# The first block by token halves, gathers of two slots for 64 tokens, and column pairs on TensorE

## Reference

```python
# first block, cut
h = rmsnorm(x, ln_mix_g) * (1 + sc1) + sh1
q, kc, vc, ksl, vsl, kw, vw, gts, cb, cc, ch = split(h @ w_in)
o_attn = nsa_mixer(...)                     # per query block: compressed, selected, window
o_conv = cb * causal_conv3(cc * ch)
mixed = concat([rmsnorm(o_attn, g), rmsnorm(o_conv, g)])
x = x + gt1 * (mixed @ w_out)
h2 = rmsnorm(x, ln_ffn_g) * (1 + sc2) + sh2
# peer_ffn(h2): q = h2 @ w_q; s = q . sub_keys  (8 heads x 2 halves x 128 keys)
# top 16 of each half, top 16 of their 256 sums -> expert number and softmax weight g
u = expert_u[ec]                            # 128 tokens x 128 slots x 1024
act = gelu(einsum('cd,ced->ce', xc, u))
out = einsum('ce,ced->cd', gc * act, expert_v[ec])
x = x + gt2 * out
# second block: attention with rotary embedding and a gated delta net, on the normed x
```

## Time and profile before

| | us |
|---|---|
| median of 3 runs (lowest, highest) | 1513.19 (1512.33, 1513.9) |
| the profiled execution, its own time | 1513.2 |
| its span, first to last instruction | 1511.3 |
| PE busy / DVE busy / ACT busy / POOL busy | 1281.6 / 746.8 / 477.1 / 368.4 |
| mean granted TensorE clock | 0.948 |

### The profile page before, as it was taken

How to read it: one execution, slowest core, us unless ns; L and a number is a source line. 1 busy time by engine, 2 the same in 40 slices (tenths; PEclk the granted TensorE clock), 3 DMA queues, 4 the chain that set the end, 5 groups by cost and what they waited for, 6 DMA issues and landing times.

```text
span 1511.3 us, 13142 instructions
## 1 busy us (share of the span) xinstructions
PE 1281.6 (85%) x4744; PEld 771.6 (51%) x4744; DVE 746.8 (49%) x1657; ACT 477.1 (32%) x1224; POOL 368.4 (24%) x285
## 2 busy tenths in 40 slices
PE   5899877887798887878889878699997789999896
PEld 1688545652233323223333322255775679999782
DVE  2313552748986696555544454511667764431212
ACT  1022220134343334344243333312785441111101
POOL 0688100134353454344334444100000000000000
PEclk9898888899999999999999999999998989999999
DMA  9775400599999999999999999645322130204130
GB/s 338 288 257 212 160 14 0 215 393 421 421 390 418 410 417 407 422 420 422 421 384 387 391 423 421 264 141 194 112 94 74 56 112 1 83 32 164 56 111 28
DMA packets 90827, 376.92 MB, mean 249 GB/s; under 512 B 6307, under 2 KB 8524, under 8 KB 57932
## 3 DMA queue, kind: packets, MB, share of 16 engines
q0 software_dynamic: 36864, 268.45, 43.3%
q1 hardware_dynamic: 52112, 103.46, 19.0%
q10 hardware_dynamic: 1788, 4.19, 0.9%
HBM read 375.02 MB, written 1.06 MB: 249 GB/s over the span
## 4 chain that ended last, share of the span: by engine, by line
PE 49%; DMA 21%; DVE 18%; ACT 8%; issue 2%; POOL 1%; SPq 0%; DVEq 0%; ACTq 0%; POOLq 0%
PE ps L87 49%; DMA AR<-in_puv,idx 19%; DVE AR L87 9%; DVE acc L87 3%; ACT L87 3%; DMA W<-in_w_mod 2%; ACT acc L87 2%; DVE tok L87 1%; ACT wv L87 1%; DVE RT L87 1%; ACT AR L87 1%; DVE hT L87 1%; ACT tok L87 1%; DVE junk L87 1%; POOL AR L87 1%
## 5 line engine op out<-in xcount | busy, mean ns | idle before, releaser
L87 PE MATMUL ps<-AR,acc 128*128 128x512 f32 x1024 | 500.5, 626 | 114.7 <-ACT acc L87 111.0
L87 DVE CUSTOM_DVE_ANT_0 AR<-AR,tok 128x1024 f32<-128x1024 f32 x256 | 312.6, 1223 | 219.0 <-DMA AR<-in_puv,idx 217.9
L87 POOL DMA_INDIRECT AR<-in_puv,idx x256 | 276.3, 1079 | 526.5 <-PE ps L87 390.3
L87 PEld LDWEIGHTS ps<-AR,acc 128*128 128x128 f32 x1024 | 183.8, 194 | 429.1 <-ACT acc L87 266.0
L87 PE MATMUL ps<-hT,W 128*128 128x256 f32 (+2 forms) x1504 | 323.1, 375 | 3.2 <-ACT hT L87 2.2
L87 PEld LDWEIGHTS ps<-hT,W 128*128 128x128 f32 (+1 forms) x1504 | 271.9, 198 | 46.1 <-issue 7.4
L87 ACT ACTIVATE wv<-av 128x1 f32<-128x1 f32 x256 | 51.5, 201 | 350.2 <-DVE av L87 349.9
L87 ACT ACT_TABLE_LOAD x90 | 115.5, 1283 | 16.8 <-issue 15.3
L87 ACT ACTIVATE acc<-K,wv 128x128 f32<-128x128 f32 x256 | 102.8, 402 | 8.4
L87 PE MATMUL ps<-W,hT 128*128 128x512 f32 (+3 forms) x288 | 95.2, 487 | 0.0
L87 ACT ACTIVATE wv<-wv,gw 128x1 f32<-128x1 f32 x256 | 75.4, 294 | 8.3
(11 more groups left out here) (199 smaller groups left out, 1035.8 us busy)
## 6 DMA issues: line engine op xcount, KB each, us to landing
W<-in_w_in SPq DMA_DIRECT2D x25, 2048.0 KB, 7.9
W<-in_w_mod SPq DMA_DIRECT2D x12, 2048.0 KB, 16.9
W<-in_w_out SPq DMA_DIRECT2D x2, 2048.0 KB, 10.3
W<-in_wq SPq DMA_DIRECT2D x2, 2048.0 KB, 10.3
AR<-in_puv,idx POOLq DMA_INDIRECT x256, 12.7
W<-in_wba SPq DMA_DIRECT2D x2, 2048.0 KB, 7.8
W<-in_wbb SPq DMA_DIRECT2D x2, 2048.0 KB, 7.7
W<-in_wo SPq DMA_DIRECT2D x2, 2048.0 KB, 7.8
```

What stands on the lines that cost most here:

```text
L87: ins = f(*args, **kw)
```

## The change

The first block's tail is done for tile 0 alone before the first gather, and the other tile's work stands in the gather loop.

- **Split work.** `conv_step`, the two norms, `attn_add` and the query projection exist per tile (`norm_root`, `conv_mix`, `attn_root`, `attn_mix`, `q_norm`), `scores` is cut into `scores_mm`, `scores_add` and `weigh`, and the compressed scores of tile 1 into `cmp_s1` to `cmp_s3`. Before the loop stand tile 0, unit 4, and the scores of unit 5. The rest of tile 1 is the generator `half1`, one list of pieces after each of the first 19 pairs.
- **Routing** goes by one head, one head, then two at a time (tile 1: always two). The last part of each group (`pieces`) is put off by some steps, and lays `idx` and `gwp` out anew by small matmuls (`spread`).
- **Gather layout.** One indirect DMA still brings 128 rows, but for 64 tokens and two slots: partitions 0 to 63 hold slot 2m of these tokens, 64 to 127 slot 2m+1. A pair of gathers (g = 0, 1) covers 128 tokens. `q_back` writes `h2` twice, once for each partition half, into `H2`.
- **Column pairs.** `dg` is 128x64 (`fold`, two identities on top of each other, times the weights), and PE sums a gather's two slots into 64 PSUM partitions, g = 0 into 0 to 63 and g = 1 into 64 to 127, in turn.
- **Slots.** The loop starts with 5 gather slots (`ring`), as `AR` still holds tile 1's data behind them, and gets two more when `route(1)` starts. Three of the 5 are free at once, two only after `conv_mix(1)`. A pair takes two slots and gives both back after its last matmul.
- **Pace.** Routing advances by 5 steps per pair for p < 20, by 8 after. The two `mod_row(3, n)` come together, when `route(1)` is through. Bias rows are loaded one by one, as their space falls free.

```diff
-        steps += [lambda: (scores(0), compress(0)), lambda: (scores(1), compress(1)), lambda: turn_p(0), compress_k, compress_v,
-                  lambda: (scores(2), turn_p(1)), lambda: cmp_scores(0), lambda: cmp_scores(1),
+        steps += [lambda: (scores(0), compress(0), weigh(0)), lambda: (scores(1), compress(1), weigh(1)), lambda: turn_p(0),
+                  compress_k, compress_v, lambda: (scores(2), turn_p(1), weigh(2)), lambda: cmp_scores(0),
                   lambda: (cmp_turn(0, 0), cmp_turn(0, 1)),
-                  lambda: (cmp_add(0, 0), cmp_add(0, 1), pv_(0), pv_(1), turn_p(2), scores(3)),
-                  lambda: (cmp_turn(1, 0), cmp_turn(1, 1)), lambda: (cmp_add(1, 0), cmp_add(1, 1))]
...
+        def q_back(a, g, k4, free):
+            c = a * 128 + g * 64
+            b = ps.take()
+            for kk in range(4):
+                for q in range(2):
+                    t = PE(mm, b.t[q * 64:q * 64 + 64, kk * 128:kk * 128 + 128], hT[:, 4 * k4 + kk, c:c + 64], ident,
+                           start=True, stop=True, after=b.old + t_hx[a])
+            e = A(act, H2[a][g][:, k4 * 512:k4 * 512 + 512], b.t[:, :], ACT.Copy, after=[t] + free)
+            b.free = [e]
+            t_h2[a].append(e)
+
...
+        def spread(src, nh, after):
+            b = ps.take()
+            for q in range(2):
+                for g in range(2):
+                    t = PE(mm, b.t[q * 64:q * 64 + 64, g * 8 * nh:g * 8 * nh + 8 * nh], ident[:, g * 64:g * 64 + 64],
+                           src.rearrange("p (m q) -> p q m", q=2)[:, q, :], start=True, stop=True, after=b.old + after)
+            b.free = []
+            return b, t
...
-            for h0, nh in ((0, 2), (2, 2), (4, 4)):
-                bs, t = banks[h0 // 4]
-                hp = [(h % 4, h, p_) for p_ in range(2) for h in range(h0, h0 + nh)]
+            late, sc_ = [], {}
+            groups = (((0, 1), (1, 1)), ((0, 2),))[a] + ((2, 2), (4, 2), (6, 2))
...
+        qp = mixT
+        for j in range(4):
+            conv_step(j, 0)
+        turn_p(3)
+        pv_(2)
+        b2 = ps.take()
+        for n in range(4):
+            t_mc.append(mod_cols_sum(b2, 4 * n, *t_ms[n]))
+        sh2, sc2, t_m2 = mod_affine(b2, t_mc[3], 24, V_LNF, 16)
+        norm_root(("c", 0), nrm[:, 0, :], cbT[:, :, 0:P], t_oc[0])
+        pv_(3)
+        conv_mix(0)
+        for n in range(2):
+            t_g1.append(mod_row_sum(2, n, *t_ms[4 + n]))
+        attn_root(0)
+        attn_mix(0)
+        attn_mm(0, 0)
+        for j in range(4):
+            conv_step(j, 1)
+        attn_add(0, 0)
+        scores(4)
+        attn_mm(0, 1)
+        weigh(4)
+        attn_add(0, 1)
+        turn_p(4)
+        q_norm(0, [])
+        q_project(0, 0)
+        routes = [route(0, [])]
+        t_fold = V(tt_, fold[:, :], ident[:, 0:64], ident[:, 64:128], ADD, after=[t_in])
         while (0, 0) not in t_idx or (0, 0) not in t_gw:
             advance(routes[0], 1)
-        attn_add(1, ob1)
-        queries(1)
-
+        norm_root(("c", 1), nrm[:, 1, :], cbT[:, :, P:2 * P], t_oc[1])
+        for g in range(2):
+            for k4 in range(2):
+                q_back(0, g, k4, [t_hx[0, "x"]] if g == 0 else [stage[3, "T"]])
+        pv_(4)
+        q_project(0, 1)
+        scores(5)
...
+        ring = [[n, [t_gel[0], t_gel[1], t_c["k"], t_c["v"]] + (t_mix[1] + [t_mixfree[0]] if n > 2 else [])] for n in range(5)]
...
+        def half1():
+
+            yield [lambda: weigh(5), lambda: q_project(0, 2), lambda: scores_mm(6)]
+            yield [lambda: scores_add(6), lambda: turn_p(5), lambda: cmp_s1(1)]
+            yield [lambda: cmp_s2(1), lambda: weigh(6), lambda: pv_(5), lambda: scores_mm(7)]
+            yield [lambda: cmp_s3(1), lambda: scores_add(7), lambda: turn_p(6), lambda: q_project(0, 3)]
+            t_keys[1] = SP.dma(nc.sync.dma_start, s_k, kT_sb[1], keys3, after=[stage[6, "T"]])
+            yield [lambda: weigh(7), lambda: pv_(6), lambda: cmp_turn(1, 0)]
+            yield [lambda: turn_p(7), lambda: cmp_turn(1, 1)]
+            load_row(0, [stage[7, "T"]])
+            yield [lambda: pv_(7)]
+            yield [lambda: cmp_add(1, 0), lambda: cmp_add(1, 1), lambda: attn_root(1)]
+            late_t["dg"] = stage[7, "e"]
+            t_dgs = [t for f in dg_free for t in f]
+            yield [lambda: attn_mix(1, t_dgs)]
+            yield [lambda: attn_mm(1, 0, 0, 4)]
+            yield [lambda: attn_mm(1, 0, 4, 8)]
+            yield [lambda: attn_mm(1, 1, 0, 4), lambda: attn_add(1, 0)]
+            yield [lambda: attn_mm(1, 1, 4, 8)]
+            yield [lambda: attn_add(1, 1), lambda: q_norm1(1)]
+            yield [late_keys, lambda: q_norm2(1, [t_keyfree[3]])]
+            for m in range(4):
+                yield [lambda: q_project(1, m)]
+
...
+        def fetch(a, c):
+            while (a, c // 16) not in t_idx:
+                advance(routes[0], 1)
+            n, free = ring.pop(0)
             return n, G.dma(nc.gpsimd.indirect_dma_start, gsem[n], GB[:, n, :], None, puv,
-                            bass.IndirectOffsetOnAxis(ap=idx[:, a, q:q + 1], axis=0),
-                            after=slot_free[n] + [t_idx[a, q // 16]])
+                            bass.IndirectOffsetOnAxis(ap=idx[:, a, c:c + 1], axis=0),
+                            after=free + [t_idx[a, c // 16]])
...
+        dg1 = acc[:, 0, 0:512].rearrange("p (n t) -> p n t", n=NDG)
+
+        def dg_at(d):
+            return dg1[:, d, :] if "dg" in late_t else mixT[:, d // 2, P + 64 * (d % 2):P + 64 * (d % 2) + 64]
...
+            ws = []
+            for g in range(2):
+                c = 2 * m + g
+                w = av[:, a, c:c + 1]
+                e = A(act, w, w, ACT.Gelu_apprx_tanh, after=[t_dot[p, g][1]])
+                e = A(act, w, w, ACT.Copy, scale=gwp[:, a, c:c + 1], after=[e, t_gw[a, m // 8]])
+                d = (2 * p + g) % NDG
+                ws.append((d, A(act, dg_at(d), fold[:, :], ACT.Copy, scale=w,
+                                after=[e, t_fold] + dg_free[d] + ([late_t["dg"]] if "dg" in late_t else t_mc))))
             for c in range(2):
-                e = PE(mm, E[a][c].t[:, :], dg[:, d, :], GB[:, n, D + c * 512:D + c * 512 + 512], start=(q == 0),
-                       stop=(q == 127), after=E[a][c].old + [td])
-            dg_free[d] = [e]
-            slot_free[n] = [e]
+                for g in range(2):
+                    n = t_dot[p, g][0]
+                    d, td = ws[g]
+                    e = PE(mm, E[a][c].t[64 * g:64 * g + 64, :], dg_at(d), GB[:, n, D + c * 512:D + c * 512 + 512],
+                           start=(m == 0), stop=(m == 63), after=E[a][c].old + [td])
+                    if c == 1:
+                        dg_free[d] = [e]
+                        ring.append([n, [e]])
...
+        h1 = half1()
+        for p in range(P):
+            a, m = p // 64, p % 64
...
+            for g in range(2):
+                n, t = fetch(a, 2 * m + g)
+                t_dot[p, g] = n, V(ttr, GB[:, n, 0:D], GB[:, n, 0:D], H2[a][g], 1.0, 0.0, MUL, ADD,
+                                   av[:, a, 2 * m + g:2 * m + g + 1], after=[t] + t_h2[a])
+                t_lastdot[a] = t_dot[p, g][1]
+            e = combine(p)
+            u = 2 * p + 1
+            for todo_ in h1:
+                for f in todo_:
+                    f()
+                break
+            advance(routes[0], 5 if p < 20 else 8)
+            if (0, 7) in t_gw and len(routes) == 1 and len(t_qp[1]) == 4:
+                t_eq["hold"] = [late_t["dg"]]
+                eqbuf[0] = acc[:, 1, :].rearrange("p (h s j) -> p h s j", h=4, s=16)
+                ring.append([5, [stage[7, "O"], t_mix[1][-1]]])
+                ring.append([6, [stage[7, "O"], t_mix[1][-1], t_eq["last"]]])
+                routes.insert(0, route(1, [t_idx[0, 7], t_gw[0, 7]]))
...
+            if (1, 7) in t_gw and len(routes) == 2:
+                routes.append(None)
+                load_row(3, [t_idx[1, 7], t_gw[1, 7]])
+                for n in range(2):
+                    t_g2.append(mod_row(3, n))
```

524 lines of the change are left out of this document (298 added, 226 removed).

## The result

The changed kernel takes 1533.28 us (median of 4, 1524.64 to 1535.78), the kernel before 1512.76 (4 runs, 1511.48 to 1513.9). The ratio is 1.0124, interval 1.0089 to 1.0159: 20 us slower, where 4.7 faster was forecast.

The account below looks back on a forecast made before the run. The gather loop was taken as bound by DMA bytes; 255 + 150 + 144 + 95 put dot 129 at 644, and a second half of 320.5 left 4.7 us of gain: 1513.2 - 4.7 = 1508.5 us, range 1480 to 1538.

Parts of the forecast that it names:

- first dot: Start of the gather loop: first dot at 255 us, 40.5 us before the old one.
- pairs 0 to 19: Loop start with tile 1's pieces between pairs: 150 us, possibly 137 to 162.
- pairs 20 to 63: Rest of the first half: pairs 20 to 46 take 144 us, pairs 47 to 63 take 95.
- second half: Dot 129 to the last dot: 320.5 us against 326.1, pairs bearing the second block's projections a little better.
- When the first gather is issued: Work before the loop: first issue at 234.8 us, 45.5 earlier, despite 7.2 us lost by moved projection calls.
- A pair: PE's eight records per pair of gathers: 2.3 us with column halves overlapping, 3.5 if none does.
- The small ring: Loop with 5 slots: cycle of 11.0 us for two pairs, 5.5 a pair against 4.98 of DMA.
- Tile 1's work between pairs: Pairs 0 to 19, heavy pieces costing their serial chain: 36.8 + 28.8 + 29.6 + 16.5 + 38.5 = 150 us.
- The two `mod_row`: Pairs 47 to 63: 13.9 us of PE in one piece, hidden by up to 7 outstanding gathers; uncovered up to 14.
- Overlap: Rival in pairs 0 to 19: pieces fill PE's and ACT's waits, about 120 us there, 1479 in all; chance 0.22.
- No column overlap: Rival in PE's products: 8 paces per pair, 28 us more over 24 chain-bound pairs, 1536; chance 0.12.
- The clock: Rival: PE falls to 1.2 GHz in waits, 1.05 us more in each of the first 24 pairs, 1533; chance 0.17.

Follow-up runs that it names:

- e3_gap: Changed kernel with an empty step put before `cmp_turn(0, ...)`, so projection calls stand again ahead of its transposes: 1523.67 us, ratio 1.0071 to the kernel before.
- e5_ring5: Changed kernel with 5 gather slots throughout, slots 5 and 6 never given to the ring: 1639.17 us, ratio 1.0886 to the kernel before.
- e11_ring5_filler: Kernel with 5 slots throughout, plus two extra 512-column PE calls behind each pair's products from pair 64 on: 1625.36 us, ratio 1.0784 to the kernel before.
- e16_before_loop_ring7: Changed kernel with all tile 1 pieces before the first pair, sixth slot from pair 0, seventh soon after: 1566.40 us, ratio 1.0366 to the kernel before.
- e4_filler: Changed kernel with two extra 512-column PE calls ahead of each of the first 64 pairs' products, `spread` banks held until read: 1535.37 us, ratio 1.0149.
- e7_halves_apart: Changed kernel with a pair's four PE calls ordered g, then c, column halves not in turn: 1527.98 us, ratio 1.0122 to the kernel before.
- e15_apart_halves: Kernel with early ring, empty step, norm at routing's pace and pieces every second pair, plus calls ordered g, then c: 1509.7 us, ratio 1.0008.

## Why the prediction was wrong

The stages, as forecast and as measured (mean of the two profiled executions of the changed kernel, 1524.64 and 1532.7):

| | forecast | measured | difference |
|---|---|---|---|
| first dot | 255 | 258.5 | +3.5 |
| pairs 0 to 19 | 150 | 157.8 | +7.8 |
| pairs 20 to 63 | 239 | 247.7 | +8.7 |
| second half | 320.5 | 325.6 | +5.1 |
| behind dot 256, against before | 0 | -4.0 | -4.0 |

The sum is 21, and that is the miss. The forecast kept a gain of 4.7 us between a start worth 40 and losses of 36, so four sizes that were each 1 to 5% too small turned its sign. The step that failed is the price of the early pairs, 150 and 239 against 157.8 and 247.7: a pair with a light piece was put at 5.5, and PE's products at 2.3 us throughout, so that half rate stood among the rivals and at nothing in the sum. That the early terms missed by no more than 5% is in part luck, as the groups below show.

*When the first gather is issued: nearly right.* 238.9 against 234.8, 4.1 us of the miss. The loss by the moved projection calls was put at 7.2 us and is 7.1 (run e3_gap). The 19 us between first issue and first dot were put at 20.

*A pair: right,* 2.15 us for eight records, overlap also with 128 rows. The rule on independent tiles in the Trainium skill, "TensorEngine Tiling (Array Packing)", Key Properties, agrees with that row.

*The small ring: mis-sized.* 5.5 us a pair, measured 6.25 where nothing else runs, and 5.61 with the clock at 1.00 (runs e5_ring5 and e11_ring5_filler). So most of the 0.75 is half rate. In 24 pairs it would be 18 us, an estimate and an upper one, as pairs with heavy pieces may hide it. That 5.5 is so near to 5.61 is luck in part: I took the 6.25 us of a gather into idle queues, and in those pairs a gather took 6.8 to 10.4 us from issue to dot (run e11_ring5_filler).

*Tile 1's work between pairs: mis-sized,* 150 against 157.8, by errors that nearly cancel. From dot to dot of the changed kernel, the first four pairs, which carry the exps, took 30.8 us (put at 36.8), the four with half an `attn_mm` half 23.9 (28.8), the four with a `q_project` piece 22.8 (29.6), and pair 14 18.4 (16.5; 362.68 to 381.11). Against that the other seven, put at 5.5 each and 38.5 together, took 61.9. Three of them make it: pair 7 with 13.7 (waits of 4.4 and 5.2 us for gathers that were issued late), pair 8 with 12.7 (`attn_mix(1)` waits 4.31 us for PE in DVE's queue ahead of the dots, as the score addition 4.26 in pair 1, and a landed gather that waits keeps its slot), and pair 19 with 11.8 (a wait of 7.2 us for a gather while two weight loads ran).

*Pairs 20 to 63: mis-sized,* 239 against 247.7. I let DMA be the bound from pair 24; the stretch from 416 to 480 still ran at 389 GB/s (4 us), six gathers are under way for the first time at 450 us, behind pair 24, and from 480 on DMA was full, at 406 to 419 GB/s. With the ring grown early and no pieces it was full from pair 4 on (run e16_before_loop_ring7). The two `mod_row` were hidden, as said.

*Second half: the gain of 5.6 was not there.* The second half took 323.5 to 328.0 us in the runs with 7 slots, before 326.1: column pairs bear the bursts of the second block's projections no better. The 4.0 us gained behind dot 256 were not forecast, and no run explains them.

*The rivals.* Overlap (dot 129 before 630) is refuted. No column overlap is refuted by the rows. The clock's number, 1533, was met, and its mechanism is there: half rate did come (0.86 and 0.76 in the first stretches, eight records in 4.5 us on the chain that ended last), and where it could be measured it costs 0.64 us a pair and not 1.05. In 24 pairs that would be 15 us, an estimate, of the 16.5 that pairs 0 to 63 missed. But in the early pairs themselves it is not shown: run e4_filler lengthened pairs 0 to 19 with its own calls and won 2 to 5 us in pairs 20 to 29, and runs e7_halves_apart and e15_apart_halves hardly changed the clock there. The pieces' and the clock's parts also overlap, since slow products are one reason why pieces wait. What stays open is how the 45 us of idle DMA time divide between ring, pieces and clock; a kernel with tile 1's pieces and 7 slots from pair 0 could not be tried, as tile 1's data lies in those slots.

## What to carry to other kernels

A transfer loop that is always full (here 411 GB/s over the first half) can only be started earlier, and that is worth the shift only if it is full from then on: here a start 37.6 us earlier was followed by 45 us' worth of idle DMA engines in the first 30 pairs. Work strung into such a loop should not stand ahead of the instruction that frees a slot, on any in-order queue. What won the time back here was an earlier start, a ring that grows early, a bulk piece spread, and then heavy pieces in every second turn only: 24 us together. A bulk piece cost nothing by itself where seven gathers were under way (the two `mod_row`). When a forecast is a small difference of large terms, its range is the sum of their errors, and the sign should be given little.
